# A weight ring whose four slots start 32, 64, 128 and 256 bytes off the 2,048-byte lines, in a two-layer encoder kernel

## The reference

```python
def swiglu(h, w_in, w_out):
    gate, up = jnp.split(h @ w_in, 2, axis=-1)
    return (jax.nn.silu(gate) * up) @ w_out
...
for l in range(DEPTH):
    x = x + 0.5 * rmsnorm(swiglu(rmsnorm(x, g[0]), ffn_w_in[l, 0], ffn_w_out[l, 0]), g[1])
    h = rmsnorm(x, g[2])
    m = mla(h, ...) if l % 2 == 0 else hgrn2(h, l, ...)
    x = x + rmsnorm(m, g[3])
    x = x + 0.5 * rmsnorm(swiglu(rmsnorm(x, g[4]), ffn_w_in[l, 1], ffn_w_out[l, 1]), g[5])
```

## Time and profile before

| what | value |
|---|---|
| time, median of 3 runs | 2031.92 us (2031.26 to 2036.8) |
| the profiled execution's own time | 2032.52 us |
| its span, first to last instruction | 2030.7 us |
| mean granted TensorE clock | 0.998 |
| PE busy | 99% of the span, 11,116 matmuls |
| PE weight loads busy | 82% |
| DVE / ACT / POOL busy | 46% / 35% / 33% |
| HBM traffic | 176 MB read, 88 GB/s over the span |

### The profile page before, as it was taken

The page is one execution under the profiler, slowest core; times in us unless marked ns, Lnnn a source line. Parts: engine busy times, 40 slices in busy tenths (PEclk is TensorE's granted clock), DMA queues, the critical chain, the costliest instruction groups (busy, mean ns, idle before and its releaser), DMA issues.

```text
span 2030.7 us, 28276 instructions
## 1 busy us (share of the span) xinstructions
PE 2019.4 (99%) x11116; PEld 1672.9 (82%) x11116; DVE 936.4 (46%) x1222; ACT 715.1 (35%) x969; POOL 668.2 (33%) x298
## 2 busy tenths in 40 slices
PE   9999999999999999999999999999999999999998
PEld 7888888888888888888888888888888888888886
DVE  6433421588384333116533411476766776344212
ACT  5222232455342222224222222374754642222221
POOL 4444444220224444442444444200000024444442
PEclk9999999999999999999999999999999999999999
DMA  4232234200222332332223233222212123233332
GB/s 166 93 103 94 91 98 133 94 22 1 73 83 93 96 101 90 96 99 98 83 95 101 93 93 96 81 93 74 74 63 74 53 73 104 93 97 99 96 97 78
DMA packets 53362, 179.46 MB, mean 88 GB/s; under 512 B 5920, under 2 KB 8224, under 8 KB 53280
## 3 DMA queue, kind: packets, MB, share of 16 engines
q1 hardware_dynamic: 52848, 176.73, 27.5%
q10 hardware_dynamic: 432, 1.57, 0.2%
HBM read 176.18 MB, written 2.10 MB: 88 GB/s over the span
## 4 chain that ended last, share of the span: by engine, by line
PE 96%; DVE 2%; ACT 1%; issue 1%; DVEq 0%; ACTq 0%
PE psum L620 28%; PE psum L622 27%; PE psum L621 27%; PE psum L776 1%; PE psum L777 1%; PE psum L782 1%; PE psum L984 1%; PE psum L723 1%; PE psum L1091 1%; ACT prob L1576 0%; PE psum L729 0%; PE psum L802 0%; PE psum L808 0%; PE psum L805 0%; PE psum L1171 0%
## 5 line engine op out<-in xcount | busy, mean ns | idle before, releaser
L556 POOL TENSOR_TENSOR w_lo<-raw,w_hi 128x1024 fp32r<-128x1024 f32 (+1 forms) x276 | 649.5, 2356 | 1299.5 <-ACT w_hi L1388 1299.5
L620 PE MATMUL psum<-xg_hi,w_hi 128*128 128x512 f32 x1735 | 682.2, 393 | 1.0 <-DVE xg_lo L2198 0.5
L622 PE MATMUL psum<-xg_hi,w_lo 128*128 128x512 f32 x1735 | 675.4, 389 | 0.0
L621 PE MATMUL psum<-xg_lo,w_hi 128*128 128x512 f32 x1735 | 675.3, 389 | 0.0
L1388 ACT ACTIVATE w_hi<-raw 128x1024 fp32r<-128x1024 f32 (+1 forms) x332 | 343.1, 1037 | 839.7 <-DMA raw<-w_up 462.9
L620 PEld LDWEIGHTS psum<-xg_hi,w_hi 128*128 128x128 f32 x1735 | 325.7, 188 | 70.2 <-issue 1.6
L622 PEld LDWEIGHTS psum<-xg_hi,w_lo 128*128 128x128 f32 x1735 | 325.6, 188 | 68.4
L621 PEld LDWEIGHTS psum<-xg_lo,w_hi 128*128 128x128 f32 x1735 | 325.8, 188 | 67.0 <-issue 1.2
L620 PE MATMUL psum<-hid_hi,w_hi 128*128 128x512 f32 x704 | 273.9, 389 | 0.0
L621 PE MATMUL psum<-hid_lo,w_hi 128*128 128x512 f32 x704 | 273.9, 389 | 0.0
L622 PE MATMUL psum<-hid_hi,w_lo 128*128 128x512 f32 x704 | 273.9, 389 | 0.0
(11 more groups left out here) (248 smaller groups left out, 1614.5 us busy)
## 6 DMA issues: line engine op xcount, KB each, us to landing
raw<-w_up SPq DMA_DIRECT2D x172, 512.0 KB, 3.5
raw<-w_down SPq DMA_DIRECT2D x64, 512.0 KB, 3.5
raw<-w_hgrn SPq DMA_DIRECT2D x48, 512.0 KB, 3.6
raw<-w_down SPq DMA_DIRECT2D x32, 384.0 KB, 3.1
raw<-w_mla SPq DMA_DIRECT2D x16, 512.0 KB, 3.5
raw<-w_up SPq DMA_DIRECT2D x16, 128.0 KB, 4.1
xt<-x_t SPq DMA_DIRECT2D x8, 256.0 KB, 4.3
out<-xt SPq DMA_DIRECT2D x8, 256.0 KB, 2.1
```

What stands on the lines that cost most here:

```text
L556: pool.tensor_tensor(w_lo[slot][:, 0:n], raw[slot][:, 0:n], w_hi[slot][:, 0:n].bitcast(F32), ALU.subtract).then_inc(w_ready, 1)
L620: first = pe.matmul(ps, w_hi[slot][:, at:at + n], hi, start=start, stop=False)
L621: pe.matmul(ps, w_hi[slot][:, at:at + n], lo, start=False, stop=False)
L622: return first, pe.matmul(ps, w_lo[slot][:, at:at + n], hi, start=False, stop=stop)
```

## The change

The four ring slots start 32, 64, 128 and 256 bytes further on than before. Within a slot nothing moves: `w_hi` still lies 4,096 bytes after `raw`. The slab of the ring grows by 256 bytes, which pushes the small tensors behind it (`cols` to `variance`) up by 256 bytes. Arena slots, activations, temporaries and constants stay where they were.

```diff
 RING = 4
 LINE = 2048
+STAGGER = (32, 64, 128, 256)
...
-        ring_at = slab("ring", RING * 2 * TILE * 4)
+        ring_at = slab("ring", RING * 2 * TILE * 4 + STAGGER[-1])
...
-        slots = [tile_slot(n, ring_at + n * 8 * TILE) for n in range(RING)]
+        slots = [tile_slot(n, ring_at + n * 8 * TILE + STAGGER[n]) for n in range(RING)]
```

## The result

| | before | after |
|---|---|---|
| median of the runs | 2031.98 us (2031.26 to 2036.8, 4 runs) | 2067.66 us (2065.78 to 2070.41, 4 runs) |
| ratio | | 1.017, 95% interval 1.0158 to 1.0182 |
| profiled execution, span | 2030.7 us | 2064.0 us |
| granted clock | 0.998 | 0.999 |

The change makes the kernel 1.7% slower. I had said no measurable change, 2032.0, with a range up to 2036.0.

The account below looks back on a forecast made before the run. PE was taken to bound the kernel, with a matmul in flight nearly throughout. All terms were 0 except 0.1 us at the first entry: 2032.5 + 0.1 = 2032.6 us, stated as 2032.0 for the median, range 2029.0 to 2036.0.

Parts of the forecast that it names:

- What bounds it: Whole kernel: PE has a matmul in flight for 2019.4 of 2030.7 us, at full granted clock in all 40 slices.
- Item 1: PE's matmul pace on ring weights: taken as 0; ends minus 13.3 ns and plus 2 ns on each of 7,500 matmuls.
- Item 2: PE's weight load from ring slots: at most 2 ns longer, covered by some 115 ns of spare, so 0.
- Items 3, 4 and 5: ACT, POOL and DVE on ring tiles: 0; steady-state DMA: 0; DMA at the first entry: 0.1 us.
- item 5: DMA at the first entry, fourth tile's piece, no spare: 0.1 us taken, from 0.49 us gained to 3.4 us lost.
- The rule on descriptors: DMA writes into three slots: 17 transactions per row instead of 16, about 0.2 us per landing, hidden; 0.1 to 0.3 at entry.
- The slower one: L620 to L622: weight load from an odd start reaches the path, 2 ns each, 15 us, 2047 us; chance 4%.
- The faster one: PE matmuls: the extra 13.3 ns is a clash of two aligned reads; staggering saves up to 100 us, 1932 us; chance 4%.
- no change: Whole kernel: time stays within the 0.3%, 6 us, that a measurement can tell; chance 89%.
- The test that I proposed: Changed profile: L620 to L622 start 226.7 ns apart in all slots; wrong if 0.8 ns off in three or four.

Follow-up runs that it names:

- other offsets: The changed kernel with its four ring slots 96, 160, 192 and 224 bytes past a line instead of 32, 64, 128 and 256: 2075.21 us.
- everything moved: Kernel before the change, with ring, arena and activations all shifted to 64 past a multiple of 256: 2034.35 us against 2033.1, ratio 1.0006.
- one slot off: The changed kernel with ring slots at 0, 64, 256 and 256 bytes past a line: 2045.73 us against 2034.55 for the kernel before, ratio 1.0059.
- half-way runs: Two runs against the kernel before (2035.52 us): weight halves given separate starts per slot, 2067.02 us; only column half `xg_lo` moved, by 192 bytes, 2043.76 us.

## Why the prediction was wrong

**What bounds it** was right, and it is why the miss hurts: PE is the path from end to end, so a few nanoseconds on each of 7,500 matmuls arrive at the end almost in full. I had priced exactly that, 7.5 us for each nanosecond. The one slip is the clock: a 9 in a slice of the page means 90% or more, and in two of the slices the granted clock was at half for 3.4 us.

**Item 1, the matmul pace, is the step that failed.** I took 0 and it was 4.6 ns per matmul, averaged over the slots (5.0 to 6.7 ns in three of them, 0 in one), 34.5 us. The zero rested on the fillers of L723, "whose operands already lie off the lines", and L1162 beside them. I looked at each operand's distance from a line, and not at the two against each other. The filler takes its weights and its columns from the same place in `const`, both 128 past; L1162 has 0 and 1,024, which is 0 modulo 256. Both rows are of operands in phase, the one relation that costs nothing, so they could not show what the change does. The same goes for the observation that the pace was equal for weights 0, 512, 1,024 and 1,536 past a line: those are all one phase. My upper end of 2 ns came from the weight load's own duration and was no bound on the pace; it would have given 15 us, and the stated range left even that out.

A row of an operand pair out of phase did stand in the trace of before, and it would have misled me too. At the end L1355 multiplies `xt` by the identity in `const`, on a line and 128 past one:

```profile
2018.65 1.02 PE L1355 MATMUL psum<-xt,const 128*128 128x512 f32 x2
```

One such matmul lasts 0.59 us, so the second started 0.43 after the first. The fillers on `t_a`, plain float32 too, in phase and with 256 columns, start 0.216 us apart once the clock is up. Twice that is the same 0.43: for plain float32 the phase of 128 cost nothing that can be seen.

**Item 2, the weight load:** it stayed at 188 ns and its cover of 115 ns held, as said. It was no protection, since the cost isn't in the duration of the load. That its reads hold up the stream is the account that fits the runs; no profile shows it directly.

**Items 3, 4 and 5** held. POOL, DVE and the landings of whole tiles are as before; the 128 KB pieces of the entry land in 4.4 us against 4.1, and PE doesn't wait for them. PE does start its first real matmuls later, at 6.98 against 6.44 us, but that isn't item 5: the fillers ahead of them took 6.17 us in place of 5.59 in the chain. They start 0.43 us apart to the last, where before the last ones were 0.22 apart: the clock rose later to its higher level, at 7.1 us against 5.9. In the other runs it rose anywhere from 4.5 to 7.1 us.

```profile
1.20 6.17 PE psum L724 x14
```

The rule on descriptors that begin off 256 bytes (the Trainium skill, DMA: Bandwidth & Descriptors, How a descriptor splits into AXI transactions) isn't borne out here, and as it speaks of reads it isn't refuted either: the landing of 512 KB is 3.5 us in both profiles, where my estimate by the rule was up to 0.2 more. With all four slots off the multiples (other offsets, everything moved) it was 3.6, but so it was in the run with one slot off.

**The rivals.** The slower one, at 4%, had the right lines, L620 to L622, and named as its second condition "where its reads hold up the moving ones". That is the condition that fits what the runs show; its price, 15 us, was under half of the 33. The faster one had the relation of PE's two reads, with the sign reversed: I supposed that equal phase was the clash and that a stagger would free it. Equal phase is the free case. What I held against it, that two streams at different rates "pass each other whatever their first byte", is refuted: the pace does depend on the first bytes, by 2.2 to 7.5 ns. With the relation in hand and no row on its sign, "faster by up to 100 us" at 4% and "slower by 15" at 4% were both far too low against 89% for no change. A change that puts 7,500 instructions of the bounding engine in a relation that the trace doesn't contain deserved more weight on the unknown and an upper end from the mechanism.

**The test that I proposed** did its work: "starts 226.7 ns apart, in tiles of all four slots alike", and wrong if the pace differs by 0.8 ns in three of four slots. It differed by 5 to 6.7 ns in three.

## What stays open

Shown, for rounded float32 matmuls of 128x128 weights and 512 columns with the weights loaded for each, is that the step depends on the difference of the two start addresses modulo 256, and not on where either lies or on what other engines do. Not shown is why. The half-way runs disagree on how the parts add (4.2 ns for one load out of three, 2.2 for one stream out of three, and the latter spread over all three matmuls). The order of the steps by difference has no shape that I can explain, 192 being mild above all. I also can't say whether the 13.3 ns that every matmul in phase has above the 213.3 ns that the prediction takes for 512 columns has to do with the weight loads; none of the twelve differences removed it. The kernel's other dtypes and widths were not varied.

## What to carry to other kernels

Where TensorE is the path and reloads its weights for every matmul, give the stationary and the moving operand start addresses that agree modulo 256 bytes; here, with rounded float32, a disagreement of even 4 bytes cost 5.7 ns on 226.7, 2.5%. For plain float32 the one row out of phase showed no cost, and other types weren't run. Where either of them lies is free, so a pad in the wrong place between them is enough to lose it, and shifting all by the same amount loses nothing. When a layout change is judged from a trace, ask for each row called in as a likeness in what relation its operands stand to each other, and read the pace from starts by slot: here no wait, no clock and no duration of another engine gave the loss away.

## What the runs showed that I had not expected

- The pace of TensorE depends on how the start addresses of its two operands stand to each other: 226.7 ns per matmul of 512 columns in phase, 228.9 to 234.2 out of phase, with POOL's and ACT's times per tile and the landings as before. The Trainium skill (SBUF — State Buffer, Who interferes with whom) has the two read ports of the array as independent. The trace disagrees as far as these rounded float32 matmuls go: their pace isn't independent of how the two reads stand to each other.
- The extra is deterministic. In slot 1 the steps alternate between 230.9 and 235.8 ns (means over the tiles, by place in the tile), and every tile of that slot does the same.
- Moving all weights of the 7,900 matmuls, the activations and the temporaries off every 256-byte multiple cost nothing measurable (1.0006, 0.9996 to 1.0015); a POOL subtraction took 2,354 ns and one of DVE 1,242, as before.
